# Pairs of half-array matmuls issued one head after the other instead of side by side

## What is computed

```python
# differential attention, 8 heads, two score maps per head (dh = 64)
s = einsum('bhiqd,bhikd->bhiqk', qb, k)              # i = 0, 1
p = softmax(where(mask, s, -inf), axis=-1)           # causal
a = p[:, :, 0] - lam * p[:, :, 1]
out = einsum('bhqk,bhkv->bhqv', a, v)

# stick-breaking attention, 16 heads (dh = 64), strictly causal
z = einsum('bhqd,bhkd->bhqk', qb, kb) * scale
log1m = where(mask, log_sigmoid(-z), 0)
excl = cumsum(log1m, reverse) - log1m                # over keys
a = where(mask, exp(log_sigmoid(z) + excl + suffix), 0)
acc = acc + einsum('bhqk,bhkd->bhqd', a, vb)
```

## Time and profile before

| | |
|---|---|
| median of three runs | 1442.56 us |
| the profiled execution, its own time | 1442.56 us |
| its span in the trace | 1440.7 us |
| TensorE busy (matmuls) | 1374.8 us, 95% of the span |
| VectorE busy | 937.0 us, 65% |
| ScalarE busy | 664.8 us, 46% |
| mean granted TensorE clock | 0.983 |

### The profile page before, as it was taken

The page is one execution under the profiler, slowest core; times in us unless marked ns, Lnnn a source line. Parts: engine busy times, 40 slices in busy tenths (PEclk is TensorE's granted clock), DMA queues, the critical chain, the costliest instruction groups (busy, mean ns, idle before and its releaser), DMA issues.

```text
span 1440.7 us, 20830 instructions
## 1 busy us (share of the span) xinstructions
PE 1374.8 (95%) x8456; PEld 1207.1 (84%) x8456; DVE 937.0 (65%) x1128; ACT 664.8 (46%) x809; POOL 81.6 (6%) x150
## 2 busy tenths in 40 slices
PE   5999899999999899999799999999999999999996
PEld 1797799998787679999698878899998987899996
DVE  4697676875797776555675345677677434677674
ACT  1543444444546454444434354554455457554452
POOL 1111100100111110000100010000000000000000
PEclk9899999999999899999999999999999999999998
DMA  9786267864695246555365434454553541454530
GB/s 369 265 345 254 100 238 286 310 233 176 244 357 202 91 181 243 198 178 177 116 209 199 161 132 175 147 204 176 180 196 123 207 144 49 157 204 176 179 143 30
DMA packets 46092, 279.23 MB, mean 194 GB/s; under 512 B 5200, under 2 KB 5200, under 8 KB 18880
## 3 DMA queue, kind: packets, MB, share of 16 engines
q1 hardware_dynamic: 33264, 231.57, 44.4%
q0 software_dynamic: 12752, 46.57, 8.7%
HBM read 277.07 MB, written 1.05 MB: 193 GB/s over the span
## 4 chain that ended last, share of the span: by engine, by line
PE 89%; DVE 5%; ACT 2%; issue 1%; DMA 1%; POOL 1%; SPq 0%; POOLq 0%; DVEq 0%; ACTq 0%
PE ps L1566 42%; PE ps L1603 13%; PE ps L1605 13%; PE ps L1604 13%; PE ps L1665 1%; DMA ada<-in_ada_w 1%; DVE h_lo L986 1%; PE ps L1627 1%; POOL rstd L499 1%; PE ps L2005 1%; PE ps L1638 1%; DVE x L1027 1%; DVE h_hi L985 1%; ACT h L600 1%; DVE xn L1023 0%
## 5 line engine op out<-in xcount | busy, mean ns | idle before, releaser
L932 DVE TENSOR_TENSOR w_lo<-raw,w_hi 128x2048 fp32r<-128x2048 f32 x210 | 479.9, 2290 | 213.1 <-ACT w_hi L575 212.2
L575 ACT ACTIVATE w_hi<-raw 128x2048 fp32r<-128x2048 f32 x210 | 400.8, 1911 | 336.6 <-PE ps L1566 289.7
L1603 PE MATMUL ps<-h_hi,w_hi 128*128 128x256 f32 x1536 | 437.2, 285 | 6.3 <-DVE h_lo L986 5.6
L1605 PE MATMUL ps<-h_hi,w_lo 128*128 128x256 f32 x1536 | 435.3, 283 | 0.0
L1604 PE MATMUL ps<-h_lo,w_hi 128*128 128x256 f32 x1536 | 435.3, 283 | 0.0
L1603 PEld LDWEIGHTS ps<-h_hi,w_hi 128*128 128x128 f32 x1536 | 293.5, 191 | 11.7 <-issue 6.6
L1604 PEld LDWEIGHTS ps<-h_lo,w_hi 128*128 128x128 f32 x1536 | 293.5, 191 | 2.0
L1605 PEld LDWEIGHTS ps<-h_hi,w_lo 128*128 128x128 f32 x1536 | 293.5, 191 | 0.0
L1566 PE MATMUL ps<-w_hi,h_hi 128*128 128x512 f32 x448 | 151.8, 400 | 1.0 <-DVE h_lo L986 1.0
L1566 PE MATMUL ps<-w_hi,h_lo 128*128 128x512 f32 x448 | 148.4, 392 | 0.0
L1566 PE MATMUL ps<-w_lo,h_hi 128*128 128x512 f32 x448 | 148.2, 392 | 0.0
(11 more groups left out here) (249 smaller groups left out, 1114.8 us busy)
## 6 DMA issues: line engine op xcount, KB each, us to landing
raw<-in_stream SPq DMA_DIRECT2D x210, 1024.0 KB, 4.9
ada<-in_ada_w POOLq DMA_DIRECT2D x80, 512.0 KB, 6.3
ada<-in_ada_w SPq DMA_DIRECT2D x8, 512.0 KB, 13.5
raw<-in_ada_w SPq DMA_DIRECT2D x8, 512.0 KB, 15.8
row<-in_gate_b POOLq DMA_DIRECT2D x3, 512.0 KB, 3.5
x<-in_x SPq DMA_DIRECT2D x1, 1024.0 KB, 10.7
retc<-in_retc POOLq DMA_DIRECT2D x1, 1024.0 KB, 5.3
out<-xn SPq DMA_DIRECT2D x2, 512.0 KB, 2.7
```

The costliest lines, as they stand in the source:

```text
L575: act.activation(w_hi[:, s, :], raw[:, s, :], ACT.Copy).then_inc(hi_done[s], 1)
L932: dve.tensor_tensor(w_lo[:, s, :], raw[:, s, :], w_hi[:, s, :].bitcast(f32), ALU.subtract)\
L1603: pe.matmul(out, wh, h_hi[:, kt, :], start=kt == 0, stop=False)
L1605: last = pe.matmul(out, wl, h_hi[:, kt, :], start=False, stop=kt == KT - 1)
```

## The change

In three functions the order in which TensorE's instructions are issued is changed. Before, each kind of matmul is issued for both halves (maps or heads) before the next kind. After, all of one half's matmuls are issued, and then all of the other's. The instructions, their operands, their number, the semaphores and the order of the functions stay the same.

```diff
 def d_scores(h):
-    half = [(slice(i * DDH, (i + 1) * DDH), d_bank(h) + i) for i in range(2)]
-    for f, b in half:
+    for i in range(2):
+        f, b = slice(i * DDH, (i + 1) * DDH), d_bank(h) + i
         pe.matmul(ps[:, b, 0:T], d_qt[f, h, P:T], d_kt[f, h, :], start=True, stop=True)
-    for f, b in half:
         pe.matmul(ps[:, b, T:T + P], d_qt[f, h, 0:P], d_kt[f, h, 0:P], start=False, stop=True,
                   skip_group_check=True)
-    for f, b in half:
         last = pe.matmul(ps[:, b, P:3 * P], maskr[:, 0:P], maskr[:, P:3 * P], start=False, stop=True,
                          skip_group_check=True)

 def s_scores(p):
-    half = [(slice(i * SDH, (i + 1) * SDH), s_bank(p) + i) for i in range(2)]
-    for f, b in half:
+    for i in range(2):
+        f, b = slice(i * SDH, (i + 1) * SDH), s_bank(p) + i
         pe.matmul(ps[:, b, 0:T], s_k[f, p, 0:P], s_q[f, p, :], start=True, stop=True)
-    for f, b in half:
         pe.matmul(ps[:, b, T:T + P], s_k[f, p, P:T], s_q[f, p, P:T], start=False, stop=True,
                   skip_group_check=True)
-    for f, b in half:
         for first in (0, T):
             last = pe.matmul(ps[:, b, first:first + P], maskr[:, 0:P], maskr[:, 3 * P:4 * P],
                              start=False, stop=True, skip_group_check=True)

 def s_output(p):
-    half = [(slice(i * SDH, (i + 1) * SDH), 2 * p + i, s_b[:, p % 3, 0, i, :]) for i in range(2)]
-    for f, h, a in half:
+    for i in range(2):
+        f, h = slice(i * SDH, (i + 1) * SDH), 2 * p + i
+        a = s_b[:, p % 3, 0, i, :]
         pe.matmul(ps[f, so_bank(p), 0:T], s_v[:, 0, h * SDH:(h + 1) * SDH], a[:, 0:T], start=True, stop=False)
-    for f, h, a in half:
         last = pe.matmul(ps[f, so_bank(p), P:T], s_v[:, 1, h * SDH:(h + 1) * SDH], a[:, T:T + P],
                          start=False, stop=True)
```

## The result

The changed kernel takes 1466.03 us, the median of four runs (1459.67 to 1471.15), against 1442.14 us for the kernel before (1441.64 to 1443.08): a ratio of 1.0154 with a 95% interval from 1.0118 to 1.0191, and 23.9 us between the medians (whose own ratio is 1.0166). The forecast was 1456.4, with a range up to 1460.0. Its sign is right and its size is not: 13.9 us forecast, 23.9 measured. The second thing to see is the spread: 11 us among the changed kernel's runs and 1.4 among those of before. With 19 more runs of the changed kernel it is larger still: the 23 lie between 1453.77 and 1471.15 us around a median of 1465.97, five of them inside the forecast's range.

A forecast was written before the change was run, and what follows sets the result against it. TensorE was taken to bound the stick-breaking attention, a chain through three engines the differential one. 1442.56 us plus 11.9 (stick-breaking) and 2.0 (differential) gave 1456.4 us, range 1454.1 to 1460.

The forecast's parts named there:

- The clock: Differential attention: the new order fills the first idle time at half clock but not the second; no term put on it.
- 2.0 us: Differential attention: sum of the delays at its start, after which the loop runs at VectorE's pace; bounds 0 and 4.0.
- The bound above: Differential attention: 4.0 us if a stretch at half clock falls into the loop, which has no slack left on TensorE.
- The rival on the clock: Differential attention: denser work keeps the full clock, at most 6.1 us comes back, 1437 us; chance 0.02.
- second sign of being wrong: Differential attention: the loop slows to TensorE's pace by more than it hides.
- The rival of exposed loads: Score functions: a lone half can't load behind its own passes, 0.66 us per call, 1461.7 to 1467.0 us; chance 0.03.
- Outputs: 4.0 us: `s_output`: second head starts only beside the first's last pass, 0.59 us more per pair of heads, partly covered; 4.0 us.
- The rival with the outputs free: `s_output`: outputs overlap more or their cost is hidden, only the scores pay, 1452.5 us; chance 0.06.
- s_scores: 7.9 us: Stick-breaking attention: eight `s_scores` calls, all on TensorE's path, 0.99 us more each, 7.9 us.
- Weight loads: Row-tiled scores: loads into the same half lie behind its passes, nothing charged; by the skill's rule about 10.6 us more.
- The start of the differential attention: Before the loop: no cover for the longer scores, so L1873 starts at 459.1 instead of 457.57, 1.5 us late.
- Alternate streams: Half-array passes run twice as fast alone, so a call costs only 0.3 to 0.4 us; 1446.3 us; chance 0.07.

The follow-up runs named there:

- `d_scores` alone: Only `d_scores` issued half by half as in the change, against the kernel before: 1457.59 us against 1441.43, ratio 1.0123.
- `s_output` alone: Only `s_output` issued half by half as in the change, against the kernel before: 1441.60 us against 1441.43, ratio 1.0001.
- the masks last: Changed kernel with the full-array masks of both score functions moved behind both halves: 1442.04 us against 1441.43 for the kernel before, ratio 1.0005.
- five heads half by half: Kernel before with `d_scores` half by half for heads 3 to 7 only, heads 0 to 2 in pairs: 1450.62 us against 1441.65, ratio 1.006.

## Why the prediction was wrong

**The clock: the step that failed.** "The new order fills the first idle time but not the second; I put no term on it." I read a fall of the clock as the answer to TensorE's idling, since both falls in the earlier trace rows come with idle time, and took it that a busier TensorE would rather help. So the differential part got 2.0 us, with a loop that "runs at VectorE's pace"; alone it measured 16.2. The runs show TensorE busy for 6.20 of 6.20 us ahead of the fall (changed kernel), and 37.00 of 37.00 while it lasted (`d_scores` alone), with turns of 6.10 us in place of 3.51; full-array passes added to the same scores kept the clock full. The price is the difference 16.2 - 4.9 = 11 us or more, since the 4.9 contain the added work. The bound above (4.0 us, "a stretch at half clock falls into the loop") allowed for one stretch. It did name the missing slack, but I didn't follow the loop on: while the clock is low TensorE sets the turn, and with lone halves in it the clock stayed low until the scores were through. That TensorE sets the turn isn't enough for that: with pairs in the loop it was busy for 10.30 of 10.30 us at half clock, and the clock came back. The rival on the clock had the right place with the wrong sign. The forecast had the clock full around 459 to 463 us, where it was 0.50, and its second sign of being wrong, a loop at TensorE's pace, came true.

**The sum.** Two misses partly cancel: 14.2 us too little in the first attention, 3.8 too much for the outputs. The rival of exposed loads had 1467.0 us, 1 us from the measured median; that is chance, since its loads cost nothing (below) and the time is the clock's.

**Outputs: 4.0 us, measured 0.2 and no different from 0.** The step was that the second head starts only beside the first head's last pass. The runs with `s_output` alone and with the masks last show that matmuls for another half of the array start without waiting for those ahead of them in the queue. The rival with the outputs free was right on this; its 1452.5 us were not, for want of the clock's term. The Trainium skill (TensorE: Matmul & The Clock Gate, Part 3) says that matmuls start and end strictly in program order, and my step agreed with it. Here the lines L2015 and L2016 speak against that, and so does the first pass to the mask in 0.86 us for both maps with the masks last.

**s_scores: 7.9 us, measured 7.8.** The terms held: 0.99 us per call in the changed kernel's timeline, and 7.95 us in its whole attention at full clock. What makes them is the mask between the halves, not the order of the halves.

**Weight loads.** I charged a lone half nothing for its later loads, against the Trainium skill's rule (TensorE: Matmul & The Clock Gate, Part 3) that a load overlaps only with matmuls of another row group. The same part of the Trainium skill also has loads into a background buffer pulled ahead of matmuls under way, which I had left out. The part of a lone half took 0.85 us, the same as a pair's: the row was right.

**The start of the differential attention**: 1.5 us late forecast, 1.45 in the trace. The 2.0 us of this part at full clock were not measured by themselves. The two traced executions that hold the full clock through a loop of lone halves both have added work in it. The run of the changed kernel at a mean clock of 0.983 took 1453.77 us, 11.6 over before; less 7.8 for `s_scores` that would leave nearly 4 us for this part, if its clock was full there, which no trace shows.

**Alternate streams** (1446.3 us) fell: lone halves take as long as pairs in each part of the timeline.

## What to carry to other kernels

Here matmuls on the two halves of the array ran at the same time in either order of the queue, as long as no matmul on the full array stood between them; put what needs the full array behind both. Before counting slack as cover, count it again at half clock (here TensorE's 6.10 us against VectorE's 3.51), and above all where halves run alone: falls that lasted 3.4 and 10.3 us with pairs in the loop lasted 41.0 and more with lone halves. And full-array passes into a bank that is about to be overwritten can be cheaper than none: clearly so beside lone halves (11 us), and by about 1 us, at the edge of what can be told, where TensorE has nothing to do for a while.

## What was not expected of the hardware

A TensorE without any idle time in the profile can lose its clock and not get it back for a long time: 0.50 through 44.4 us in the changed kernel and through 41.0 with five heads half by half. Sixteen added matmuls of 512 columns, 0.64 us per head from L1852 to L1855 (468.03 to 468.67) and so 5.1 us of work, took 11 us off the time. And the second half's passes overtook those of the first in the queue, at no cost that can be measured (ratios 1.0001 and 1.0005).
